# Scores of the prompt's differential attention as four products of 128 rows from stacked operands, in place of six of 64 rows

## What is computed

```python
q = rms_norm(q.reshape(bsz, L, DIFF_HEADS, 2, DIFF_DK), q_norm) * (DIFF_DK ** -0.5)
k = rms_norm(k.reshape(bsz, L, DIFF_HEADS, 2, DIFF_DK), k_norm)
...
s = jnp.einsum('bqhzd,bkhzd->bzhqk', qblk, k) + bias[None, None]
p = jax.nn.softmax(s, axis=-1)
attn = p[:, 0] - lam * p[:, 1]
return jnp.einsum('bhqk,bkhe->bqhe', attn, v)
```

## Time and profile before

| what | value |
|---|---|
| median of three runs | 2357.3 us |
| the profiled execution, its own time | 2357.12 us |
| span from its first to its last instruction | 2355.3 us |
| TensorE (PE) busy | 2341.6 us, 99% |
| VectorE (DVE) busy | 1572.9 us, 67% |
| ACT busy | 1205.0 us, 51% |
| mean granted TensorE clock | 0.999 |
| HBM traffic over the span | 122 GB/s |

### The profile page before, as it was taken

The page is one execution under the profiler, slowest core; times in us unless marked ns, Lnnn a source line. Parts: engine busy times, 40 slices in busy tenths (PEclk is TensorE's granted clock), DMA queues, the critical chain, the costliest instruction groups (busy, mean ns, idle before and its releaser), DMA issues.

```text
span 2355.3 us, 35382 instructions
## 1 busy us (share of the span) xinstructions
PE 2341.6 (99%) x14059; PEld 2004.0 (85%) x14059; DVE 1572.9 (67%) x2579; ACT 1205.0 (51%) x2131; POOL 0.2 (0%) x4
## 2 busy tenths in 40 slices
PE   9999999999999999999999999999999999999999
PEld 6888877888889888988888888888898898888888
DVE  8999768776587776665765548859985575433332
ACT  6334455555445565545564536647874453432432
POOL 0000000000000000000000000000000000000000
PEclk9999999999999999999999999999999999999999
DMA  5446633563224664445435223333334324333332
GB/s 207 98 105 176 213 112 98 172 207 120 70 90 147 196 187 136 135 141 161 134 99 170 90 91 124 90 108 99 99 108 152 117 81 136 110 95 98 99 99 90
DMA packets 117443, 297.96 MB, mean 127 GB/s; under 512 B 20000, under 2 KB 48416, under 8 KB 116000
## 3 DMA queue, kind: packets, MB, share of 16 engines
q1 hardware_dynamic: 108720, 271.98, 37.5%
q10 hardware_dynamic: 8560, 23.73, 3.3%
HBM read 267.48 MB, written 19.79 MB: 122 GB/s over the span
## 4 chain that ended last, share of the span: by engine, by line
PE 86%; DVE 3%; ACT 1%; issue 0%; ACTq 0%
PE ps L1669 64%; PE ps L1646 5%; PE ps L1692 3%; PE ps L1651 3%; PE ps L1764 2%; PE ps L1855 2%; PE ps L1795 1%; PE ps L1828 1%; PE ps L1843 1%; DVE wlo L1619 1%; PE ps L1779 0%; PE ps L2312 0%; DVE ringP L2190 0%; PE ps L2379 0%; PE ps L1818 0%
## 5 line engine op out<-in xcount | busy, mean ns | idle before, releaser
L1614 ACT ACTIVATE whi<-wraw 128x1024 fp32r<-128x1024 f32 x430 | 451.8, 1051 | 200.5 <-PE ps L1669 125.5
L1619 DVE TENSOR_TENSOR wlo<-wraw,whi 128x1024 fp32r<-128x1024 f32 x430 | 522.2, 1217 | 6.9 <-ACT whi L1614 6.7
L1669 PE MATMUL ps<-in_hP,whi 128*128 128x512 f32 x1272 | 504.8, 397 | 1.8 <-DVE in_lP L2197 0.9
L1669 PE MATMUL ps<-in_hP,wlo 128*128 128x512 f32 x1272 | 495.7, 390 | 0.0
L1669 PE MATMUL ps<-in_lP,whi 128*128 128x512 f32 x1272 | 495.5, 390 | 0.0
L1669 PE MATMUL ps<-hid_P,whi 128*128 128x512 f32 x1008 | 310.9, 390 | 0.0
L1669 PEld LDWEIGHTS ps<-in_hP,whi 128*128 128x128 f32 x1272 | 238.9, 188 | 54.3 <-issue 2.4
L1669 PEld LDWEIGHTS ps<-in_hP,wlo 128*128 128x128 f32 x1272 | 238.8, 188 | 50.6
L1669 PEld LDWEIGHTS ps<-in_lP,whi 128*128 128x128 f32 x1272 | 239.0, 188 | 49.1 <-issue 1.4
L2119 DVE TENSOR_TENSOR x<-ps,x 128x256 f32<-128x256 f32 (+1 forms) x191 | 106.0, 555 | 250.3 <-PE ps L1669 248.1
L1669 PE MATMUL ps<-in_S,whi 128*128 128x256 f32 x1408 | 261.1, 287 | 0.0
(11 more groups left out here) (568 smaller groups left out, 3768.4 us busy)
## 6 DMA issues: line engine op xcount, KB each, us to landing
wraw<-wt SPq DMA_DIRECT2D x432, 512.0 KB, 3.6
wraw<-wt ACTq DMA_DIRECT2D x16, 512.0 KB, 4.3
k_scratch<-region_P SPq DMA_DIRECT2D x16, 256.0 KB, 3.1
v_scratch<-vtmp SPq DMA_DIRECT2D x32, 128.0 KB, 3.2
x<-x_in SPq DMA_DIRECT2D x4, 768.0 KB, 6.7
x<-x_in SPq DMA_DIRECT2D x2, 1536.0 KB, 8.1
mix_mem<-mem_in ACTq DMA_DIRECT2D x1, 2048.0 KB, 16.1
region_S<-k_scratch ACTq DMA_DIRECT2D x2, 1024.0 KB, 6.8
```

The costliest lines, as they stand in the source:

```text
L1614: nc.scalar.activation(whi[:, (n + 3) % NHI, :, :], wraw[:, ws(n), :, :], ACT.Copy).then_inc(wh.sem, 1)
L1619: nc.vector.tensor_tensor(wlo[:, ws(n), :, :], wraw[:, ws(n), :, :], whi[:, (n + 3) % NHI, :, :].bitcast(F32), ALU.subtract).then_inc(wr.s ...
L1669: last = nc.tensor.matmul(ps[:, bank(m), 0:N[prod.g]], w_[:, k, :], x_[:, k, :], start=(k == 0 and j == 0), stop=(k == KT - 1 and j == 2))
```

## The change

For the prompt, the scores of an item become two products of 128 rows for each half z in place of three of 64. One operand holds, for a half, the rounded part of q on the half's own 64 partitions and the remainder of q on the other 64; the other operand holds a part of k twice, on both halves of the partitions. The product with the rounded part of k gives hi*hi + lo*hi, that with the remainder of k gives hi*lo and, in addition, lo*lo. Everything that has to be put beside or doubled is moved by twelve transfers per head (stack_prompt), each of 64 partitions x 512 elements (128 KB), on SP's queue, in blocks of in_hP, in_lP, sq_lP, kqP_r and region_S that are free at that time (head_high, head_stack). Where the steps stand changes too: head 0's at `len(slots) - 5`, the other heads' at `queue[4 * h - 2]`, the slot of item 4h - 3. The outputs of heads 0 to 6 are written one slot later (out_of). ACT's rounding for a head waits for the transfers of the head before.

```diff
@@ -1024,8 +1024,8 @@
-                    sb("below_kq_first", [P, 3072], on=over)
-                    kq_first = sb("kq_first", [P, 2, TP], F32R, on=over)
+                    sb("below_kq_first", [P, 1024], on=over)
+                    kq_first = sb("kq_first", [P, 3, 2, TP], F32R, on=over)
@@ -1195,6 +1195,7 @@
+                    self.stacked = kq_stacked.take({"P": 192, "S": 128}[g] * DH)
@@ -1214,6 +1215,13 @@
+
+                def out_of(self, t):
+                    for h in range(DH):
+                        late = 1 if self.g == "P" and h < DH - 1 else 0
+                        if t == h * BL[self.g] + BL[self.g] - 1 + self.out + late:
+                            return h
+                    return None
@@ -1491,10 +1499,10 @@
-            attach(len(slots) - 3, [[("stack", dP, qkv, 0)]])
+            attach(len(slots) - 5, [[("stack", dP, qkv, 0)]])
...
-                queue[4 * h - 1].append(("stack", dP, qkv, h))
+                queue[4 * h - 2].append(("stack", dP, qkv, h))
@@ -1540,7 +1548,7 @@
-                    if step[0] == "stack" and step[1].g == "S":
+                    if step[0] == "stack":
@@ -1597,6 +1605,25 @@
+
+            def stack_prompt(sp, d_, qkv_, h):
+
+                to, hi, lo = [a.bitcast(F32) for a in head_stack(h)], head_high(h).bitcast(F32), kqP_r[:, :, h, :].bitcast(F32)
+                if h == 0:
+                    sp.wait_ge(gs["P"]["ssum"].sem, qkv_.stats[15].sum)
+                if h >= 3:
+                    sp.wait_ge(sc_done.sem, d_.b + BL["P"] * (h - 1))
+                sp.wait_ge(kq_high_d.sem, d_.hi + h + 1)
+                halves = (slice(0, 64), slice(64, P))
+                for zz in range(2):
+                    own, other = halves[zz], halves[1 - zz]
+                    for rows, part_, src in ((own, 0, hi[own, 0]), (own, 1, hi[own, 1]), (other, 1, hi[own, 1])):
+                        sp.dma_start(to[part_][rows, zz, :], src).then_inc(kq_stacked.sem, 16)
+                sp.wait_ge(kq_low_d.sem, d_.lo + h + 1)
+                for zz in range(2):
+                    own, other = halves[zz], halves[1 - zz]
+                    for rows, part_, src in ((other, 0, lo[own, 0]), (own, 2, lo[own, 1]), (other, 2, lo[own, 1])):
+                        sp.dma_start(to[part_][rows, zz, :], src).then_inc(kq_stacked.sem, 16)
@@ -1812,7 +1839,7 @@
-                            pe.wait_ge(kq_stacked.sem, kq_stacked.at(128 * (h + 1)))
+                            pe.wait_ge(kq_stacked.sem, a.stacked + 128 * (h + 1))
@@ -1820,13 +1847,12 @@
-                        pe.wait_ge(kq_low_d.sem, a.lo + h + 1)
-                    hi, lo, own = head_high(h), kqP_r[:, :, h, :], slice(b * P, (b + 1) * P)
-                    for j, (q_part, k_part) in enumerate(((hi, hi), (lo, hi), (hi, lo))):
-                        for zz in range(2):
-                            rows = slice(64 * zz, 64 * zz + 64)
-                            last = nc.tensor.matmul(ps[:, 3 + zz, 0:N[g]], q_part[rows, 0, own], k_part[rows, 1, :],
-                                                    start=(j == 0), stop=(j == 2))
+                        pe.wait_ge(kq_stacked.sem, a.stacked + 192 * (h + 1))
+                    q_parts, k_high, k_low = head_stack(h)
+                    for zz in range(2):
+                        for j, k_parts in enumerate((k_high, k_low)):
+                            last = nc.tensor.matmul(ps[:, 3 + zz, 0:N[g]], q_parts[:, zz, b * P:(b + 1) * P], k_parts[:, zz, :],
+                                                    start=(j == 0), stop=(j == 1))
@@ -2019,20 +2045,32 @@
-                    return (kq_first[:, :, :], in_h["P"][:, 6:8, :])[h]
-                return kqP_r[:, :, h - 2, :]
+                    return (kq_first[:, 0], in_h["P"][:, 0:2, :])[h]
+                if h < 4:
+                    return kqP_r[:, :, h - 2, :]
+                return in_h["P"][:, 4:6, :] if h == 4 else in_h["P"][:, 6:8, :]
+
+            def head_stack(h):
+
+                def slots_of(a, *at_):
+                    return [a[:, i:i + 2, :] for i in at_]
+                early_, late_ = kqP_r[:, 0], kqP_r[:, 1]
+                return {0: [sq_l["P"][:, :, :], kq_first[:, 1], kq_first[:, 2]],
+                        1: slots_of(in_l["P"], 2, 4, 6), 2: slots_of(in_h["P"], 2, 4, 6), 3: slots_of(in_l["P"], 2, 4, 6),
+                        4: slots_of(early_, 0, 2) + slots_of(late_, 0), 5: slots_of(in_l["P"], 4, 6) + slots_of(late_, 2),
+                        6: slots_of(early_, 0, 2) + slots_of(late_, 0), 7: slots_of(early_, 4) + slots_of(late_, 4, 2)}[h]
...
-                        a.wait_ge(kq_stacked.sem, kq_stacked.at(128 * h))
+                        a.wait_ge(kq_stacked.sem, d_.stacked + 128 * h)
...
-                elif h >= 2:
-                    a.wait_ge(sc_done.sem, d_.b + BL["P"] * (h - 1))
+                if h >= 1:
+                    a.wait_ge(kq_stacked.sem, d_.stacked + 192 * h)
@@ -2059,8 +2097,8 @@
-                if d_.last(t - d_.out):
-                    h = (t - d_.out) // BL[g]
+                if d_.out_of(t) is not None:
+                    h = d_.out_of(t)
...
@@ -2631,7 +2669,10 @@
-                            stack_head(sp, *stack_at[n][1:])
+                            if stack_at[n][1].g == "S":
+                                stack_head(sp, *stack_at[n][1:])
+                            else:
+                                stack_prompt(sp, *stack_at[n][1:])
```

## The result

The changed kernel takes **2360.86 us**, the median of 22 runs (2359.42 to 2364.04), against 2357.19 of before in the same job (22 runs): a ratio of **1.0017, 95% interval 1.0011 to 1.0023**. It is slower by 3.7 us. That is less than the 0.2% that I named as my bound, but outside the interval, and not the "no change" around 2357.3 that I forecast. The profiled execution took 2360.24 us around a span of 2358.5 (before: 2357.12 around 2355.3), so the two traces differ by 3.2 us and show most of it.

The account below looks back on a forecast made before the run. From item 8 on, TensorE and VectorE were both taken to be at their limit together. Terms -1.4 - 0.7 + 1.3 + 0.8 = 0.0 us left the forecast at 2357.3 us, range 2354.5 to 2361.5.

Parts of the forecast that it names:

- no change: Whole kernel: 2357.3 us, nothing a measurement can tell (0.2%, 4.7 us); chance 0.81.
- TensorE's saving: Prompt scores: four products of 128 rows replace six of 64, saving 0.18 us per item, at most 5.8 over 32.
- four products cost more than three pairs: Rival, prompt scores: the borders stay, so each item costs one step more, 7.3 us in all, 2364.5; chance 0.03.
- the ring: Head-to-head steps, items 8 to 27: TensorE's statistics wait for VectorE's remainder of squares; gain 0 (bounds 0 to 3.6 us).
- TensorE alone sets the pace: Rival, whole stage: VectorE's lag may grow, so all 32 items give 5.8 us, less 0.4 at head 1: 2351.9; chance 0.08.
- -1.4 for items 0 to 7: First eight items, before VectorE's pace binds: their score savings arrive, 8 x 0.18 = 1.4 us.
- -0.7 for items 28 to 31: Last four items, after VectorE last held TensorE: score savings of 0.7 us arrive (bounds 0 to 0.7).
- the stall of head 1: First scores of head 1: transfers land late and TensorE waits 1.3 us (0.4 to 2.7).
- late at every head: Rival, first scores of heads 1 to 7: transfers land too late, +5.7 us, 2362.9; chance 0.08.
- The output of heads 0 to 6 moves one slot later: ACT squares before rounding the output: in_lP waits 0.4 us more in two up-tile heads, 0.8 in all (bounds 0 to 4.5).

Follow-up runs that it names:

- VectorE relieved: Changed kernel with all outputs in old slots, transfers of heads 1 to 7 one slot earlier, and their q and k remainder moved from VectorE to GpSimd: 2351.66 us.
- The kernel with early transfers: Changed kernel with all outputs in their old slots and rounding, remainder and transfers of heads 1 to 7 one slot earlier: 2355.32 us.
- the order alone: Kernel before, six products and no transfers, with only the change's order: rounding a slot earlier, outputs of heads 0 to 6 a slot later: 2362.5 us.
- the run with the wait set right: Kernel before with the q and k remainder of heads 1 to 7 on GpSimd, started only after VectorE's scaling and sum (corrected index): 2356.71 us.

## Why the prediction was right or wrong

**Right: TensorE's saving.** Slots of 5.13, 0.17 to 0.18 per item. The rival that four products cost more than three pairs is out: with VectorE relieved, all 32 savings arrive.

**Right: the ring is VectorE's.** I took 0 for items 8 to 27. The kernel with early transfers goes from -1.42 at item 8 to -1.19 at item 28, with none of the 3.6 us gained, and the relieved one drops by 0.6 to 0.8 per head. The rival "TensorE alone sets the pace" is out.

**Right: -1.4 for items 0 to 7 and -0.7 for items 28 to 31**, as -1.46 and -0.62 where nothing masked them.

**Mis-sized: the stall of head 1**, 1.3 predicted, 2.16 measured, within the bounds of 0.4 to 2.7. The issue was not slow: the twelfth transfer went out at 1592.84, 7.28 us behind the start of the weight load in front of them, against the 7.6 of the working. Its landing was late: 3.9 us, where I took the sample's median of 2.9. The last row tells the landing of that one transfer alone:

```profile
1585.56 0.33 SPq L1563 DMA_DIRECT2D wraw<-wt  x1
...
1592.84 1.57 SPq L1626 DMA_DIRECT2D in_lP<-kqP_r  x1
...
DMA to landing us min/median/max: 3.9/3.9/3.9
```

The data were there at 1596.7 in place of 1596.1; TensorE began 0.1 later, and without the stall it would have been there at 1594.66, 0.14 sooner than the 1594.80 of the working. On the page, the two groups of such transfers that it lists land after 3.7 and 3.9 us by their medians.

No other head waited: the rival "late at every head" is out.

**Wrong, and the step that failed: "The output of heads 0 to 6 moves one slot later".** I took 0.4 in each of the two ring heads whose slots hold up-tiles, wrote that "in the others ACT is free in time", and so put the heads behind the ring at nothing. In the ring that was near: in_lP of heads 2 and 3 waits 0.56 and 0.55 in place of 0.37, that of the other three no longer than before, and the ring loses 0.38 against my 0.8. But the reason I gave, that both engines arrive earlier than in the old order, does not carry it: with the order alone all five heads lose, 2.95 in all. In the changed kernel VectorE lags 0.5 us more behind TensorE, and that hid 2.6 of it, which my working did not say. What I left out are heads 5 and 6. Their outputs now fall in slot 30, the last but one with scores, and in slot 34, behind the scores, where a slot takes 4.2 us. VectorE has caught up with TensorE there, and ACT is not free in time. In head 5 its rounding stands behind squares that wait for TensorE's products with v, without any eviction; in head 6 it stands behind evictions that wait for TensorE's tile, and the squares. From the rounding the chain runs on through in_lP and sq_lP to TensorE's statistics. I looked there only at the last in_lP of head 7, which was not moved. The new waits of 1.13 and 1.25, and behind the second the step in_lP itself, cost 0.78 and 1.87 us, **2.65 in place of 0**. The runs that put these outputs back, or let ACT round first, take this loss away, or 1.9 of it.

The sum as measured, by the trace: -1.46 + 2.16 + 0.38 - 0.62 + 2.69 = +3.15 us. The medians differ by 0.5 more; the runs of the changed kernel scatter over 4.6 us, and those with head 1's transfers early over 0.85.

## What to carry to other kernels

Where two engines run in step, as here, shortening one shows nothing until the other is relieved, and relieving that one alone shows next to nothing either (0.4 us): read both sides of the ring and change both. When a step is moved by one slot, go through every slot in which it lands, the last ones of the stage above all, where slots are shorter and other engines' queues are filled differently. A transfer that is planned by the median landing of other transfers may land later, here by 1.0 us: start it a slot earlier if its source and its target allow it.

## What the runs showed of the hardware that was not expected

GpSimd and VectorE held each other up by nearly whole instructions. The one-operand scaling of 128x512 took 2.41 us in place of 0.55 beside GpSimd's subtraction, which took 2.81 in place of 2.42. In the run with the wait set right, the weights' remainder, an instruction with two operands in SBUF, did the same:

```profile
1657.21 2.09 DVE L1619 TENSOR_TENSOR wlo<-wraw,whi 128x1024 fp32r<-128x1024 f32 x1
```
```profile
1655.80 2.42 POOL L2052 TENSOR_TENSOR kqP_r<-region_P,kqP_r 128x1024 fp32r<-128x1024 f32 x1 [19.23 <-DVE vtmp L2272]
```

GpSimd ends at 1658.22, and the 1.22 us of the remainder counted from there would end at 1659.44; it ended at 1657.21 + 2.09 = 1659.30. The scaling ended 0.29 behind GpSimd, less than its own 0.55. VectorE's reduction of the scores, with one operand in PSUM, ran at its usual 0.69 in between. The Trainium skill, page "SBUF — State Buffer", section "Who interferes with whom", states this as an exclusive lock on a shared pair of ports that holds for the whole instruction. These rows agree with it in the main; by a strict reading both VectorE steps would have ended somewhat later than they did, by 0.14 and 0.26 us. That GpSimd's subtraction of 128x1024 takes 2.42 us, twice VectorE's 1.22, did not matter in these runs, because nothing waited for it. When it starts mattered.
